# One 2 MB request in place of two of 1 MB for each piece of the experts' weights

## The reference

```
def swiglu(x, w1, w3, w2):
    return (jax.nn.silu(x @ w1) * (x @ w3)) @ w2

for e in range(N_EXPERTS):                       # 8 experts, D_FF = 3584
    out = out + combine[:, e:e + 1] * swiglu(xt, w1[e], w3[e], w2[e])
```

## Time and profile before

| | |
|---|---|
| median of 3 runs | 1530.22 us |
| the profiled execution | 1530.75 us, its span 1528.9 us |
| granted PE clock over the span | 0.991 |
| loads of experts' weights | 336 of 1024 KB each, median 7.6 us from issue to landing |
| experts' stage | about 545 us to 1513 us |

### The profile page before, as it was taken

The page is one execution under the profiler, slowest core; times in us unless marked ns, Lnnn a source line. Parts: engine busy times, 40 slices in busy tenths (PEclk is TensorE's granted clock), DMA queues, the critical chain, the costliest instruction groups (busy, mean ns, idle before and its releaser), DMA issues.

```text
span 1528.9 us, 23454 instructions
## 1 busy us (share of the span) xinstructions
PE 1497.9 (98%) x8803; PEld 1302.6 (85%) x8804; DVE 1233.6 (81%) x906; ACT 962.3 (63%) x693; POOL 81.6 (5%) x65
## 2 busy tenths in 40 slices
PE   9998999999999989999999999999999999999997
PEld 9987899999999868888888888888888888888885
DVE  6897866665578488888888888888888888888897
ACT  6644453333353467777777777777777777777774
POOL 1035100000000030000000000000000000000300
PEclk9998999999999999999999999999999999999998
DMA  9645788888555479999999999999999999999991
GB/s 317 197 138 159 246 313 298 296 299 314 189 195 175 149 253 396 394 368 390 367 378 373 366 391 371 366 384 370 380 382 360 381 384 355 389 373 375 372 397 62
DMA packets 212938, 483.97 MB, mean 317 GB/s; under 512 B 8810, under 2 KB 26314, under 8 KB 209820
## 3 DMA queue, kind: packets, MB, share of 16 engines
q1 hardware_dynamic: 209224, 473.67, 85.2%
q10 hardware_dynamic: 2388, 5.32, 0.9%
q0 software_dynamic: 1280, 4.33, 0.7%
HBM read 446.45 MB, written 36.87 MB: 316 GB/s over the span
## 4 chain that ended last, share of the span: by engine, by line
PE 86%; DVE 1%; DMA 1%; ACT 0%; issue 0%; DVEq 0%; SPq 0%; ACTq 0%
PE Q L2533 20%; PE Q L2486 13%; PE Q L2484 13%; PE Q L2485 13%; PE Q L2030 8%; PE Q L2031 8%; PE Q L2032 8%; PE Q L2517 2%; DMA raw<-in_moe_w 1%; PE Q L2463 0%; PE Q L2494 0%; DVE wlo L1164 0%; PE Q L2389 0%; PE Q L2417 0%; ACT yrows L1139 0%
## 5 line engine op out<-in xcount | busy, mean ns | idle before, releaser
L1164 DVE TENSOR_TENSOR wlo<-raw,whi 128x2048 fp32r<-128x2048 f32 x413 | 938.4, 2290 | 200.4 <-ACT whi L978 124.1
L978 ACT ACTIVATE whi<-raw 128x2048 fp32r<-128x2048 f32 x336 | 642.8, 1920 | 189.4 <-PE Q L2486 82.6
L2484 PE MATMUL Q<-whi,xgh 128*128 128x512 f32 x896 | 357.1, 399 | 0.1
L2486 PE MATMUL Q<-whi,xgl 128*128 128x512 f32 x896 | 353.1, 394 | 0.0
L2485 PE MATMUL Q<-wlo,xgh 128*128 128x512 f32 x896 | 352.0, 393 | 0.0
L2030 PE MATMUL Q<-xh,whi 128*128 128x264 f32 x1024 | 294.4, 287 | 3.2 <-DVE xl L1423 1.3
L2031 PE MATMUL Q<-xl,whi 128*128 128x264 f32 x1024 | 291.7, 285 | 0.0
L2032 PE MATMUL Q<-xh,wlo 128*128 128x264 f32 x1024 | 290.4, 284 | 0.0
L2486 PEld LDWEIGHTS Q<-whi,xgl 128*128 128x128 f32 x896 | 168.7, 188 | 37.6
L2485 PEld LDWEIGHTS Q<-wlo,xgh 128*128 128x128 f32 x896 | 169.0, 189 | 36.4
L2484 PEld LDWEIGHTS Q<-whi,xgh 128*128 128x128 f32 x896 | 168.8, 188 | 36.0 <-issue 0.5
(11 more groups left out here) (280 smaller groups left out, 1142.2 us busy)
## 6 DMA issues: line engine op xcount, KB each, us to landing
raw<-in_moe_w SPq DMA_DIRECT2D x336, 1024.0 KB, 7.6
raw<-in_ffn_w SPq DMA_DIRECT2D x42, 1024.0 KB, 7.6
raw<-in_hgrn_w_in SPq DMA_DIRECT2D x16, 1024.0 KB, 6.7
xg_rows<-zeros SPq DMA_DIRECT2D x6, 2048.0 KB, 10.9
y_rows<-zeros SPq DMA_DIRECT2D x6, 2048.0 KB, 11.9
raw<-in_conv_w_in SPq DMA_DIRECT2D x12, 1024.0 KB, 5.3
st<-in_state_hgrn SPq DMA_DIRECT2D x8, 512.0 KB, 4.4
raw<-in_hgrn_w_out SPq DMA_DIRECT2D x4, 1024.0 KB, 5.3
```

The source lines that it names most:

```text
L978: a.activation(bufs(q)[0], raw[:, n % RAW, PW * (q % 2):PW * (q % 2 + 1)], ACT.Copy).then_inc(hi_done, 1)
L1164: v.tensor_tensor(low, raw[:, slot, PW * half:PW * (half + 1)], high.bitcast(F32), ALU.subtract).then_inc(lo_done, 1)
L2484: t_.matmul(out, xgh[:, kt, :], high[:, w], start=(kt == 0), stop=False)
L2486: mm = t_.matmul(out, xgl[:, kt, :], high[:, w], start=False, stop=(kt == DT - 1))
```

## The change

The experts' pieces are no longer issued by `chunk` but by `piece`: one request for all 2 MB, once both halves of the slot are free (`lo_done` of half 2p-5, which is the condition that the second half's request had). Its landing is told by one semaphore of the slot, `raw_loaded[slot][0]`, and ACT waits for that one before either half. The other stages keep their two requests.

```
+            def piece(n, src, slot):
+
+                k, w = src.shape[1], src.shape[2]
+                sp.wait_ge(lo_done, n * 2 - (2 * RAW - 2))
+                sp.dma_start(raw[:, slot, :].rearrange("p (k w) -> p k w", k=k), src
+                             ).then_inc(raw_loaded[slot][0], 16)
+
...
-                chunk(n, expert(moe_w1, e, 0, DT)[:, :, 0:FW], 0)
-                chunk(n + 1, expert(moe_w3, e, 0, DT)[:, :, 0:FW], 1)
+                piece(n, expert(moe_w1, e, 0, DT)[:, :, 0:FW], 0)
+                piece(n + 1, expert(moe_w3, e, 0, DT)[:, :, 0:FW], 1)
...
-                    chunk(m, expert(moe_w1, e, 0, DT)[:, :, cols], 2)
-                    chunk(m + 1, expert(moe_w3, e, 0, DT)[:, :, cols], 0)
-                    chunk(m + 2, expert(moe_w2, e, i * 4, 4), 1)
+                    piece(m, expert(moe_w1, e, 0, DT)[:, :, cols], 2)
+                    piece(m + 1, expert(moe_w3, e, 0, DT)[:, :, cols], 0)
+                    piece(m + 2, expert(moe_w2, e, i * 4, 4), 1)
...
-                    act.wait_ge(raw_loaded[n % RAW][q % 2], loads * 16)
+                    act.wait_ge(raw_loaded[n % RAW][0], loads * 16)
```

More of the change, by code:

```diff
@@ L470, in body @@
                     cols = bass.ds(i * FW + FW, FW)
-                    chunk(m, expert(moe_w1, e, 0, DT)[:, :, cols], 2)
-                    chunk(m + 1, expert(moe_w3, e, 0, DT)[:, :, cols], 0)
-                    chunk(m + 2, expert(moe_w2, e, i * 4, 4), 1)
+                    piece(m, expert(moe_w1, e, 0, DT)[:, :, cols], 2)
+                    piece(m + 1, expert(moe_w3, e, 0, DT)[:, :, cols], 0)
+                    piece(m + 2, expert(moe_w2, e, i * 4, 4), 1)
                 if ahead:
                     rows_in(k + 1, row + SLOTS)
-                    chunk(n + (JOB - 1), expert(moe_w1, e + 1, 0, DT)[:, :, 0:FW], 2)
-                    chunk(n + JOB, expert(moe_w3, e + 1, 0, DT)[:, :, 0:FW], 0)
-                    chunk(n + (JOB + 1), expert(moe_w2, e, 4 * (FB - 1), 4), 1)
+                    piece(n + (JOB - 1), expert(moe_w1, e + 1, 0, DT)[:, :, 0:FW], 2)
+                    piece(n + JOB, expert(moe_w3, e + 1, 0, DT)[:, :, 0:FW], 0)
+                    piece(n + (JOB + 1), expert(moe_w2, e, 4 * (FB - 1), 4), 1)
                 else:
-                    chunk(n + (JOB - 1), expert(moe_w2, e, 4 * (FB - 1), 4), 2)
+                    piece(n + (JOB - 1), expert(moe_w2, e, 4 * (FB - 1), 4), 2)
                 if not isinstance(k, int):
```

## The result

The change makes the kernel slower: 1545.16 us (median of 4 runs, 1541.80 to 1547.78) against 1530.22, a ratio of 1.0097 (95% interval 1.0079 to 1.0116), +14.9 us. I had forecast slower, but 1537.3 us and at most 1542.3. The profiled execution took 1544.1 us, its span 1542.3, 13.4 us more than the 1528.9 before; all that follows accounts for these 13.4.

A forecast was written before the change was run, and what follows sets the result against it. Transfers between the routing and the first down_m set PE's one stall, 5.6 us. Terms of 4.6 (start) and 2.5 (gather) on the profiled 1530.75 gave 1537.85, less 0.53 to the median: 1537.3 us, range 1532.8 to 1542.3.

The forecast's parts named there:

- the first term: Start of the experts: late piece 3 and hi's wait for all of piece 5 delay the first down_m by 4.6 us.
- my lower bound: Stall before the first down_m: +2.6 us if the added MB of piece 3 is free.
- Halves 6 and 7 do not stall PE earlier: Before the first down_m: piece 3 lands at 554.9, its lo's end at 559 and 563, in time for PE; no cost.
- The even stretch: 600 to 1400 us: a 2 MB load lands 1.1 us before its hi, and later ones are covered; zero cost.
- a cover of 10 us: Even stretch: lo of half 26 ends 10.0 us before PE uses it, so ACT's waits for late loads cost PE nothing.
- the gather: Second term, last expert: POOL's gather shares the DMA engines, later landings make two down_m late, 2.5 us in all.
- Every block pays: Rival, chance 0.06: 2 MB requests land late, PE is held to the ring's pace, 0.2 us some 48 times, 1546.9 us.
- Faster: requests cost engine time: Rival, chance 0.06: each request holds the DMA engines a fixed time, so fewer requests shorten the first stall, 1528.0 us.

The follow-up runs named there:

- e2: Kernel before, requests by half as they were, but ACT waits for both halves of a piece before copying the first: 1535.02 us, 1.0034.
- e4: Changed kernel with piece 3 alone asked for in two halves, so that half 6 is early again: 1544.26 us, 1.0097.
- e6: Changed kernel without the third product in the experts, a third less work for PE: 1534.17 us, 1.0033.
- e8: Changed kernel with each transpose of the hidden rows done three times, PE's block 17.92 us: 1584.30 us, against 1577.32 for the kernel before slowed likewise.
- e3: Changed kernel, but each piece as two 1 MB requests, asked for when the whole slot is free, ACT waiting for both landings: 1542.91 us, 1.0082.
- e5: Kernel before without the third product in the experts, a third less work for PE: 1486.59 us, 0.9718.
- e1: Changed kernel, but two 1 MB requests per piece, both asked for when the whole slot is free, ACT waiting by half: 1531.77 us, 1.0014.
- e11: Changed kernel with silu, hth and htl ahead of the second hi and lo in six of an expert's seven blocks: 1546.02 us, 1.0098.
- e12: Kernel before with hth and htl ahead of both first hi and lo in the first expert's first five blocks: 1523.22 us, 0.9957.

## Why the prediction was right in direction and wrong in size

**Right: the direction, and the first term's way.** Piece 3 is asked for at 545.37 (545.4 forecast), piece 5 at 556.66 (556.6), lands at 572.6 (573.1), its hi starts at 572.73 (573.2), and the releaser is still htl. The first down_m is 4.2 us late, where the term said 4.6. e2 bears out its larger part: the wait for the whole piece alone makes that stall 2.6 us longer, 8.27 against 5.64, as my lower bound had it (2.6).

**Wrong within the first term: "Halves 6 and 7 do not stall PE earlier".** Piece 3 landed at 556.1, 1.2 us after my 554.9, and I looked only at its weights. The silu behind its hi, 1.28 us of table load and 0.60 of work, holds the bank that PE writes next; PE waits 4.00 us at 560.08. It cost little, because it took its time out of the later stall (3.57 in place of 10.2): the two add up to 7.6, against 5.6 before. In e4 this wait is gone and the later one is 8.5, so the start gains 1.4 us by it. From the second down_m on, the start costs 3.5 us, 1.1 less than the term.

**The step that failed: "The even stretch ... A lone 2 MB takes 5.0 + 2.7 = 7.7 us, so it lands 1.1 us ahead ... Zero."** No request is alone there. At its issue the one before is on its way, and it takes 9.8 us in the median, 2.1 more than I took. With the 7.3 us until the slot asks again, the turn is as long as PE's block, and e6 shows that it stays so with a third less work for PE (17.11). I had compared one landing with one hi and a cover of 10 us, and not the turn with the block. A cover hides late landings only as long as the ring wins it back between them, and in the mean this ring wins next to nothing (17.11 against 17.17 over whole experts). So the lead wanders, as the rows of htl show, and where it came to nothing, at 1199 to 1235 us, the stretch cost 2.9 us. The 10 us were also the wrong cover. They were those of w2's weights, while every wait of PE in this stretch is for htl, and htl was only 3.7 us ahead in the kernel before.

**The term that was mis-sized: the gather, 2.5 us, measured 6.6.** The place, the releaser and the count of such waits were about right (one of 4.8 us at 1446 with 1.6 us at the low clock behind it). But I let the ring come in with its old lead less 2.7 us. It came with less: one block ahead, at 1424, htl is 0.7 us early where it was 2.2 before. The request goes out 1.5 us later than PE's own delay, all of it behind the gather's start, and takes 15.3 us in place of 11.6. In e8, where PE is slow enough for the ring to keep some lead, the wait there is 2.47 us.

**The rivals.** "Every block pays", to which I gave 0.06, came nearest to the mechanism: "PE is held to the ring's pace". Its price had the wrong form, and that its 1546.9 us lies near the measured time is chance. It is not 0.2 us in each of 48 blocks, but nothing while there is a lead, and up to whole microseconds where something comes late. My argument against it, 393 GB/s where 369 are asked for, took the rate of a ring that keeps four requests asked for, and left out what else is moved. With the experts' rows, the kernel before moves 374 GB/s from 800 to 1200 us at PE's pace; the changed ring yields 378 there with PE nearly out of its way (e6), and from 600 to 1400 us both move 377. "Faster: requests cost engine time" is refuted: half as many requests of twice the size (the change against e3) gain nothing measurable.

The Trainium skill ("DMA: Bandwidth & Descriptors", section "Rules for kernel authors") asks for at least 1 MiB a transfer where bandwidth counts; e5, with 1 MB each, holds 395 GB/s, so these runs agree that this is large enough, and larger did not help. The same section of the Trainium skill advises to issue a transfer early and to wait for it late. The change does the opposite of both, by half a piece each, and e1 to e3 put a price on it: 2.1, 5.4 and 13.3 us. The 2.0 us plus bytes at 436 GB/s that the prediction quotes stand in the Trainium skill (same page, section "Anatomy of one DMA") as a fit for transfers issued by GpSimd; the loads here are issued by SP, and the one that ran alone took 5.0 us where the fit gives 4.4.

**What stays open.** Why the changed ring yields 378 GB/s and not 395: e6 shows the dips and the fewer requests, but no run separates a request's own way to its first byte from transfer engines that finish at different times. Also argued and not shown: that the wider spread of the change (6.0 us over 4 runs; the kernel before 1.8 over 4, and 3.1 over the 17 of e1's series) comes from late landings that a thin cover no longer hides.

## What to carry to other kernels

For a ring of buffers compare the turn of a slot (request to landing, landing to last read, last read to the next request) with the consumer's time for as many pieces, and take the request's time from the crowded stretch and not from a lone one; a cover of 10 us says nothing if the turn is as long as the block. Take the consumer's own waits out of the turn first: while the consumer sets the pace, the turn equals its block whatever the slack (17.1 in both kernels here). The slack shows in how long the engine that empties the ring waits for the consumer and for loads, or in a run with less work for the consumer (e6). The unit in which a slot is freed and the unit in which its landing is told were worth more here than the size of the request: with three slots, halves instead of whole pieces were the slack. Where a stall's releaser changes when the order is changed and the time does not (e11), the releaser was only the place, so cure the supply first; where the supply has slack (e12), the order is worth changing.

## What the runs showed that I had not expected

Two conditions that cost 2.1 and 5.4 us alone cost 13.3 together. The transfers of 1 MB ran at 395 GB/s for 400 us, with no slice of 0.85 us under 376, when about four were asked for, and at 378 when 1.7 of 2 MB were (e5, e6), though the bytes asked for were not much fewer (4.4 and 3.6 MB). And PE's own waits add up to less than what they cost: behind the stall at 1446 the granted clock was 0.5 for 3.4 us, which made the next down_m another 1.6 us late.
